# A decoder layer in split fp32: one 512-column product at the start of each gate, branch, out and down unit

## The chip, the cores and the metric

The kernel runs on one core of one Trainium2 chip. The metric is the device time of one execution in microseconds. The kernel before took 1376.24 us (median of three runs, 1376.17 to 1376.32).

## The reference

One layer of a decoder, 256 tokens of 2048 channels, all in float32. The large matrix products are the input projection, three branch projections, the output projection and the three of the FFN:

```python
h = rms_norm(x, norm_mix)
qkv..., gates = split_cols(h @ w_in, IN_SPLITS)      # 3608 columns, then 3 x 2048 gate columns
y_a, y_b, y_c = three attention mixers
merged = sum_i sigmoid(g_i) * (y_i @ w_br_i)
x = x + merged @ w_out
h = rms_norm(x, norm_ffn)
x = x + (silu(h @ w_gate) * (h @ w_up)) @ w_down     # width 5632
return rms_norm(x, norm_final)
```

## The kernel before

Each float32 operand of a large product is split into a high part in the fp32r format and a low part, the rest, also in fp32r; a product is then hi x hi + hi x lo + lo x hi. The activations are stationary (blocks of 128 channels by 128 tokens, two token tiles, `TT`), the weights are the moving operand.

The work goes in units. A unit is 256 rows (two blocks, `UK`) by 512 columns (`W`) of one weight matrix, 480 columns (`WQ`) in the first part. SyncE loads it into a ring of four slots (`raw_ring`), ScalarE writes the high part (`weight_hi_ring`, L1071), VectorE the low part (`weight_lo_ring`, L1322), and TensorE waits for the low part (`lo_ready`), multiplies, and counts `unit_used` up with its last product, which frees the slot.

The order of units is written out. First 64 units of the projection (query, key, value and so on; 480 columns, 248 in the last chunk), until about 170 us. Then, from unit `U_MIX` on, 96 gate units and 24 branch units, with the attention work placed between units by `follow` and `mixer_step`, and 32 out units, until about 660 us. Then the FFN: 88 gate, 88 up and 88 down units in an order of two halves (`ffn_plan`). Gate and up units alternate, with transposes of the activations between some of them (`act_transposes`). The up units have a scheme of their own (`up_unit`, `into`, L885 to L888), in which 55 of the 88 use seven block products for eight. The last four down units are multiplied in `last_units`.

All other units go through `products` (L636). For each of two blocks k, two token tiles t and two column halves, it issues three products of 256 columns: L646 hi x hi, L647 hi x lo, L648 lo x hi, with a weight load of the stationary block before each (PEld). Both halves of a token tile go to one PSUM bank, `bank[2 * pair + t]`; the first product into a bank of a chunk carries the start flag, and the second half relies on it (L645). `straight`, through `unit`, and `ffn_unit` call `products`.

Of the kernel before, what the change touches and what calls it, by code (L numbers as in the profile page):

```python
# [20 lines left out]
P = 128  # L21
TT = 2
# [3 lines left out]
W = 512  # L26
# [26 lines left out]
UK = 2  # L53
RING = 4
UPC = KD // UK
N_QKV = -(-N_PROJ // WQ)
U_MIX = N_QKV * UPC
# [65 lines left out]
LAST_DOWN = (1, NC_D - 1)  # L123
# [12 lines left out]
def half_of(i):  # L136

    return next(h for h, (a, b) in enumerate(HALVES) if a <= i < b)
# [93 lines left out]
def build_layer(nc, x_in, norm_mix, w_in, sinks, pe_k, w1_k, w2_k, pe_v, w1_v, w2_v,  # L232
                w_br_a, w_br_b, w_br_c, w_out, norm_ffn, w_gate, w_up, w_down, norm_final, out):
    ctx = ExitStack()
    with ctx:
# [3 lines left out]
        def at(name, shape, offset, dt=F32):  # L239
            return nc.alloc_sbuf_tensor_at(name, [P] + shape, dt, offset=offset)  # L240

        def place(name, shape, dt=F32):
            n = 4
            for s in shape:
                n *= s
            n = (n + 31) // 32 * 32
            t = at(name, shape, top[0], dt)
            top[0] += n
            assert top[0] <= nc.sbuf_top, name
            return t  # L250

        raw = place("raw_ring", [RING, UK, W])
        whi = place("weight_hi_ring", [RING, UK, W], F32R)
# [48 lines left out]
        h2T_hi = at("h2T_hi", [KD, S], mid, F32R)  # L302
        h2T_lo = at("h2T_lo", [KD, S], mid + 4 * KD * S, F32R)
# [52 lines left out]
        bank = [ctx.enter_context(nc.psum_tensor(f"bank{i}", [P, W], F32)) for i in range(8)]  # L356

        def sem(name):
            return ctx.enter_context(nc.semaphore(name))
# [5 lines left out]
        unit_used = sem("unit_used")  # L365
# [266 lines left out]
        def _(pe):  # L632
            def transpose(dst, src, n=P):
                return pe.transpose(dst, src, ident[0:n, 0:n])  # L634

            def products(slot, lhs, pair, first, last, k0, width=W, tiles=tuple(range(TT)), halves=(0, 1), apart=False):  # L636

                l_hi, l_lo = lhs
                parts = [(h * Q4, (h + 1) * Q4) for h in halves] if width == W else [(0, width)]
                for k, t, (a, b) in [(k, t, part) for k in range(UK) for t in tiles for part in parts]:  # L640
                    moved = apart and t == TT - 1 and a > 0
                    dst = bank[LAST_BANK][:, 0:Q4] if moved else bank[2 * pair + t][:, a:b]
                    x_hi, x_lo = (m[:, k0 + k, t * P:(t + 1) * P] for m in (l_hi, l_lo))
                    w_hi, w_lo = (m[:, slot, k, a:b] for m in (whi, wlo))
                    opening = first and k == 0 and (a == 0 or moved)  # L645
                    pe.matmul(dst, x_hi, w_hi, start=opening, stop=False, skip_group_check=True)  # L646
                    pe.matmul(dst, x_hi, w_lo, start=False, stop=False, skip_group_check=True)  # L647
                    m = pe.matmul(dst, x_lo, w_hi, start=False, stop=last and k == UK - 1, skip_group_check=True)  # L648
                return m

            def unit(u, lhs, q, j, n, width=W):

                pe.wait_ge(lo_ready, u + 1)
                m = products(u % RING, lhs, q % 2, j == 0, j == n - 1, UK * j, width)
                m.then_inc(unit_used, 1)

            def pair_free(q):

                if q >= 2:
                    how = evac_engine(q - 2)  # L660
                    pe.wait_ge(emptied[how], evac_count(q - 2))

            def straight(u):
                q, j = CHUNK_OF[u]
                kind, i, _, n = CHUNKS[q]
                if j == 0:
                    pair_free(q)
                    if q == 1:
                        pe.wait_ge(squares, 2 * NC_D)
                if kind == "branch":  # L670
                    s = i // NC_D

                    pe.wait_ge(values_read, (CMP + 1, N_SOFT, N_SOFT + SB_HEADS)[s])
                    lhs = (yT_hi[:, s % 2, :, :], yT_lo[:, s % 2, :, :])
                elif kind == "out":
                    lhs = (hT_hi, hT_lo)
                    if i == 0:
                        pe.wait_ge(t_lo, UPC + j + 1)
                else:
                    lhs = (hT_hi, hT_lo)  # L680
                    if q == 0:
                        pe.wait_ge(t_lo, j + 1)
                unit(u, lhs, q, j, n, min(WQ, N_PROJ - i * WQ) if kind == "qkv" else W)
# [210 lines left out]
            def up_unit(u, i, j):  # L894

                def block(k, t):
                    return tuple(m[:, UK * j + k, t * P:(t + 1) * P] for m in (h2T_hi, h2T_lo))

                stop = j == UPC - 1
                if not is_seven(u):  # L900
                    for k in range(UK):
                        into(i, 3, 0, block(k, 0), quarters(u, k, 0), stop)
                        into(i, 2, 0, block(k, 0), quarters(u, k, 1), stop)
                        into(i, 2, 1, block(k, 1), quarters(u, k, 0), stop)
                        m = into(i, 3, 1, block(k, 1), quarters(u, k, 1), stop)
                    return m
                n, e = SEVEN.index(j), N_SEVEN[u] % 2
                if i == 0:
                    pe.wait_ge(h_sum_lo, n + 1)

                def total(r):
                    return tuple(m[:, n, r, :] for m in (h2S_hi, h2S_lo))

                def extra(r):
                    return tuple(m[:, e, r, :] for m in (ext_hi, ext_lo))

                into(i, 6, 0, block(0, 0), quarters(u, 0, 0), True)
                into(i, 3, 0, block(1, 0), quarters(u, 1, 0), False)
                into(i, 2, 0, total(3), quarters(u, 1, 1), False)
                into(i, 6, 1, total(1), quarters(u, 0, 1), True)  # L920
                into(i, 7, 0, total(0), extra(0), True)
                into(i, 7, 1, total(2), extra(1), True)
                return into(i, 2, 1, block(1, 1), extra(2), False)

            def ffn_unit(u):

                what, i, j = FFN[u - U_FFN]
                if what == "gate":
                    if j == 0 and i == 0:
                        pair_free(Q_FFN)  # L930
                    elif j == 0 and half_of(i) != half_of(i - 1):
                        pe.wait_ge(added, TT * (NC_D - 1))
                    elif j == 0:
                        pe.wait_ge(silu_ready, i)
                    if i == 0:
                        pe.wait_ge(t_lo, 2 * UPC + j + 1)
                    pe.wait_ge(lo_ready, u + 1)
                    products(u % RING, (h2T_hi, h2T_lo), 0, j == 0, j == UPC - 1, UK * j).then_inc(unit_used, 1)
                elif what == "up":
                    if j == 0 and i == 0:  # L940
                        pair_free(Q_FFN + 1)
                        pe.wait_ge(squares, 2 * TT * NC_D)
                    elif j == 0:
                        pe.wait_ge(up_emptied, i)
                        if half_of(i) != half_of(i - 1):
                            pe.wait_ge(added, TT * NC_D)
                    pe.wait_ge(lo_ready, u + 1)
                    up_unit(u, i, j).then_inc(unit_used, 1)
                else:
                    h, c = i  # L950
                    n, done = KD_H[h], TT * (NC_D * h + c - 1)
                    if j == 0 and c == 0:
                        pe.wait_ge(silu_ready, HALVES[h][1])
                    elif j == 0 and c == 1:
                        pe.wait_ge(up_emptied, HALVES[h][1])
                    elif j == 0:
                        pe.wait_ge(added, done)
                    if c == 0:
                        pe.wait_ge(aT_lo, 2 * (HALVES[h][0] + j // 2 + 1))
                    if i == LAST_DOWN and j >= n - RING:  # L960
                        return
                    pe.wait_ge(lo_ready, u + 1)
                    products(u % RING, (actT_hi, actT_lo), c % 2, j == 0, j == n - 1, UK * j,
                             apart=i == LAST_DOWN).then_inc(unit_used, 1)

            def last_units():

# [45 lines left out]
            for u in range(UPC):  # L1013
# [14 lines left out]
                if u == 3:  # L1028
                    pe.wait_ge(rows_ready, 48)
                    pe.wait_ge(gains_ready, 1)  # L1030
                    for a in range(1, 4):
                        m = transpose(bank[2][:, KD * a:KD * (a + 1)], rows[0:KD, a, :], KD)
# [724 lines left out]
```

## Time and profile before

| | |
|---|---|
| median of the timed runs | 1376.24 us |
| the profiled execution, its own time | 1378.64 us |
| its span, first to last instruction | 1376.9 us |
| mean granted clock of TensorE | 0.999 |
| instructions of PE: products, weight loads | 11280, 11280 |
| products of L646 with 256 columns | 2624 |

The profile is one execution of the program. PE is TensorE's products, PEld its weight loads, which overlap the products, DVE is VectorE, ACT is ScalarE. The ends of products are modelled, so that the records of neighbouring products overlap; starts are as recorded. A line of the order of time gives start, duration, engine, line of the kernel, operation, written tile and read tiles, size, count of merged instructions, and in brackets an idle time before it. "128*128 128x256" is a stationary block of 128 by 128 and 256 moving columns. In a table of stretches the count behind a busy time (x...) is of all records that lie in the stretch, those over its edges included.

### The profile page before, as it was taken

The numbers are of one execution on the slowest core, as the hardware profiler recorded it, in microseconds if no ns is written. First come the engines' busy times: TensorE is split into PE (matmuls) and PEld (weight loads), VectorE is DVE, ScalarE is ACT, GpSimd is POOL, SyncE is SP. The second block draws the span as 40 slices with busy tenths as digits, with TensorE's granted clock in tenths as the row PEclk, the third lists the DMA queues.
The fourth block names the chain that finished last, engine by engine and source line by source line (L and its number), as shares of the span: only waits on it lengthen the run. The fifth ranks groups of instructions, "written<-read, shape, count | busy, mean of one in ns | idle before, by whom it ended". The sixth has DMA issues, their size and how long they took to land.

```text
span 1376.9 us, 26434 instructions
## 1 busy us (share of the span) xinstructions
PE 1362.5 (99%) x11280; PEld 1325.5 (96%) x11280; DVE 922.5 (67%) x1192; ACT 702.5 (51%) x913; POOL 44.9 (3%) x70
## 2 busy tenths in 40 slices
PE   8999999999999999999999999999999999999997
PEld 7888999999999999999999999999999999999997
DVE  5554557667655657666787888875446778887554
ACT  6343356656545655465645554544334455545444
POOL 3000010000000110000000000000000000000111
PEclk9999999999999999999999999999999999999999
DMA  7776655444565666546556655565555565666653
GB/s 241 246 231 219 186 171 156 140 152 146 154 192 168 194 203 218 184 168 201 165 182 194 217 181 181 182 214 208 191 198 184 184 214 169 193 196 231 210 198 123
DMA packets 135264, 261.08 MB, mean 190 GB/s; under 512 B 8448, under 2 KB 25408, under 8 KB 134768
## 3 DMA queue, kind: packets, MB, share of 16 engines
q1 hardware_dynamic: 132912, 251.13, 57.0%
q0 software_dynamic: 1792, 7.57, 1.6%
q8 instruction: 86, 1.41, 0.4%
q10 hardware_dynamic: 448, 0.76, 0.2%
q14 instruction: 26, 0.21, 0.0%
HBM read 257.33 MB, written 2.10 MB: 188 GB/s over the span
## 4 chain that ended last, share of the span: by engine, by line
PE 88%; DVE 7%; ACT 2%; DMA 2%; issue 1%; ACTq 0%; DVEq 0%
PE bank L646 24%; PE bank L647 23%; PE bank L648 23%; PE bank L885 4%; PE bank L887 4%; PE bank L888 4%; DVE weight_lo_ring L1322 2%; PE bank L634 2%; DVE weight_sums_lo L1342 1%; ACT weight_hi_ring L1071 1%; DMA raw_ring<-in_w_up 1%; DVE weight_sums L1331 1%; PE bank L784 1%; DVE act_rows L1382 1%; PE bank L695 1%
## 5 line engine op out<-in xcount | busy, mean ns | idle before, releaser
L1322 DVE TENSOR_TENSOR weight_lo_ring<-raw_ring,weight_hi_ring 128x1024 fp32r<-128x1024 f32 (+2 forms) x479 | 579.9, 1221 | 319.2 <-ACT weight_hi_ring L1071 263.9
L1071 ACT ACTIVATE weight_hi_ring<-raw_ring 128x1024 fp32r<-128x1024 f32 (+2 forms) x431 | 446.2, 1047 | 343.4 <-PE bank L648 271.0
L646 PE MATMUL bank<-weight_hi_ring,hT_hi 128*128 128x256 f32 (+2 forms) x1276 | 380.9, 298 | 0.0
L648 PE MATMUL bank<-weight_hi_ring,hT_lo 128*128 128x256 f32 (+2 forms) x1276 | 375.5, 294 | 0.0
L647 PE MATMUL bank<-weight_lo_ring,hT_hi 128*128 128x256 f32 (+2 forms) x1276 | 375.5, 294 | 0.0
L646 PEld LDWEIGHTS bank<-weight_hi_ring,hT_hi 128*128 128x128 f32 x1276 | 239.8, 188 | 10.0 <-issue 3.4
L647 PEld LDWEIGHTS bank<-weight_lo_ring,hT_hi 128*128 128x128 f32 x1276 | 239.9, 188 | 6.1
L648 PEld LDWEIGHTS bank<-weight_hi_ring,hT_lo 128*128 128x128 f32 x1276 | 239.6, 188 | 6.3
L646 PE MATMUL bank<-weight_hi_ring,h2T_hi 128*128 128x256 f32 x704 | 196.5, 279 | 3.2 <-DVE weight_lo_ring L1322 3.1
L648 PE MATMUL bank<-weight_hi_ring,h2T_lo 128*128 128x256 f32 x704 | 195.3, 277 | 0.0
L647 PE MATMUL bank<-weight_lo_ring,h2T_hi 128*128 128x256 f32 x704 | 195.3, 277 | 0.0
L646 PE MATMUL bank<-weight_hi_ring,actT_hi 128*128 128x256 f32 x704 | 194.5, 276 | 0.0
L647 PE MATMUL bank<-weight_lo_ring,actT_hi 128*128 128x256 f32 x704 | 194.3, 276 | 0.0
L648 PE MATMUL bank<-weight_hi_ring,actT_lo 128*128 128x256 f32 x704 | 194.3, 276 | 0.0
L646 PEld LDWEIGHTS bank<-weight_hi_ring,h2T_hi 128*128 128x128 f32 x704 | 132.5, 188 | 4.9 <-DVE weight_lo_ring L1322 4.0
L648 PEld LDWEIGHTS bank<-weight_hi_ring,h2T_lo 128*128 128x128 f32 x704 | 132.6, 188 | 0.0
L647 PEld LDWEIGHTS bank<-weight_lo_ring,h2T_hi 128*128 128x128 f32 x704 | 132.2, 188 | 0.0
L647 PEld LDWEIGHTS bank<-weight_lo_ring,actT_hi 128*128 128x128 f32 x704 | 132.1, 188 | 0.0
L646 PEld LDWEIGHTS bank<-weight_hi_ring,actT_hi 128*128 128x128 f32 x704 | 132.1, 188 | 0.0
L648 PEld LDWEIGHTS bank<-weight_hi_ring,actT_lo 128*128 128x128 f32 x704 | 132.1, 188 | 0.0
L1068 ACT ACTIVATE weight_sums_hi<-weight_sums 128x768 fp32r<-128x768 f32 x55 | 46.6, 847 | 129.8 <-DVE weight_sums L1334 71.4
L885 PE MATMUL bank<-weight_hi_ring,h2T_hi 128*128 128x256 f32 x374 | 105.5, 282 | 0.0
(253 smaller groups left out, 1897.0 us busy)
## 6 DMA issues: line engine op xcount, KB each, us to landing
raw_ring<-in_w_in SPq DMA_DIRECT2D x96, 512.0 KB, 3.4
raw_ring<-in_w_gate SPq DMA_DIRECT2D x88, 512.0 KB, 4.3
raw_ring<-in_w_up SPq DMA_DIRECT2D x88, 512.0 KB, 4.2
raw_ring<-in_w_down SPq DMA_DIRECT2D x88, 512.0 KB, 3.9
raw_ring<-in_w_in SPq DMA_DIRECT2D x55, 480.0 KB, 4.2
raw_ring<-in_w_out SPq DMA_DIRECT2D x32, 512.0 KB, 4.0
raw_ring<-in_w_br_c SPq DMA_DIRECT2D x16, 256.0 KB, 3.9
raw_ring<-in_w_br_a SPq DMA_DIRECT2D x16, 256.0 KB, 6.8
```

The source lines that it names most:

```text
L634: return pe.transpose(dst, src, ident[0:n, 0:n])
L646: pe.matmul(dst, x_hi, w_hi, start=opening, stop=False, skip_group_check=True)
L647: pe.matmul(dst, x_hi, w_lo, start=False, stop=False, skip_group_check=True)
L648: m = pe.matmul(dst, x_lo, w_hi, start=False, stop=last and k == UK - 1, skip_group_check=True)
L695: pe.matmul(dst[:, S:2 * S], v[0], pT[:, i % 2, h, 0:S], start=True, stop=False)
L784: m = pe.matmul(bank[4 + h][:, P * t:P * (2 * t + 1)], qT[half, pr, P * t:P * (t + 1)], keys[half, 0:P * (t + 1)], start=True, stop=True)
L885: pe.matmul(dst, l_hi, r_hi, start=(i, b) not in opened, stop=False, skip_group_check=True)
L887: pe.matmul(dst, l_hi, r_lo, start=False, stop=False, skip_group_check=True)
L888: return pe.matmul(dst, l_lo, r_hi, start=False, stop=stop, skip_group_check=True)
L1068: act.activation(ext_hi[:, n % 2, :, :], t_sum[:, :, :], ACT.Copy)
L1071: act.activation(whi[:, s, :, 0:width(u)], raw[:, s, :, 0:width(u)], ACT.Copy)\
L1322: dve.tensor_tensor(lo, w, hi.bitcast(F32), ALU.subtract).then_inc(lo_ready, 1)
```

## The change

`products` gets a flag, `whole`. With it, the unit begins with one hi x hi product of all 512 columns for the first block and the first token tile, and the two hi x hi products of 256 columns that it stands for are left out. The other 22 products follow in their old order. The flag is set for all units from `U_MIX` on that go through `unit`, for the FFN's gate units, and for the down units, but not in the up units, the projection's units and `last_units`.

```diff
-            def products(slot, lhs, pair, first, last, k0, width=W, tiles=tuple(range(TT)), halves=(0, 1), apart=False):
+            def products(slot, lhs, pair, first, last, k0, width=W, tiles=tuple(range(TT)), halves=(0, 1), apart=False, whole=False):

                 l_hi, l_lo = lhs
                 parts = [(h * Q4, (h + 1) * Q4) for h in halves] if width == W else [(0, width)]
+                if whole:
+                    pe.matmul(bank[2 * pair][:, :], l_hi[:, k0, 0:P], whi[:, slot, 0, :], start=first, stop=False,
+                              skip_group_check=True)
                 for k, t, (a, b) in [(k, t, part) for k in range(UK) for t in tiles for part in parts]:
...
-                    pe.matmul(dst, x_hi, w_hi, start=opening, stop=False, skip_group_check=True)
+                    if not whole or k > 0 or t > 0:
+                        pe.matmul(dst, x_hi, w_hi, start=opening, stop=False, skip_group_check=True)
                     pe.matmul(dst, x_hi, w_lo, start=False, stop=False, skip_group_check=True)
                     m = pe.matmul(dst, x_lo, w_hi, start=False, stop=last and k == UK - 1, skip_group_check=True)
                 return m
...
-                m = products(u % RING, lhs, q % 2, j == 0, j == n - 1, UK * j, width)
+                m = products(u % RING, lhs, q % 2, j == 0, j == n - 1, UK * j, width, whole=u >= U_MIX)
...
-                    products(u % RING, (h2T_hi, h2T_lo), 0, j == 0, j == UPC - 1, UK * j).then_inc(unit_used, 1)
+                    products(u % RING, (h2T_hi, h2T_lo), 0, j == 0, j == UPC - 1, UK * j,
+                             whole=u >= U_MIX).then_inc(unit_used, 1)
...
-                             apart=i == LAST_DOWN).then_inc(unit_used, 1)
+                             apart=i == LAST_DOWN, whole=u >= U_MIX).then_inc(unit_used, 1)
```

## Rows read from the trace of the kernel before

**Rows 1.** The page: engines (busy, share, instructions) and the span in 40 slices.
```profile
span 1376.9 us, 26434 instructions
PE 1362.5 (99%) x11280; PEld 1325.5 (96%) x11280; DVE 922.5 (67%) x1192; ACT 702.5 (51%) x913; POOL 44.9 (3%) x70
...
PEclk9999999999999999999999999999999999999999
DMA  7776655444565666546556655565555565666653
```

**Rows 2.** Waits of PE: who waited for whom, us in total, times, longest.
```profile
PE bank L646 <- DVE weight_lo_ring L1322: 3.1, 7, 1.1
```

**Rows 3.** The page's groups: busy us, mean ns of one, idle before.
```profile
L646 PE MATMUL bank<-weight_hi_ring,hT_hi 128*128 128x256 f32 (+2 forms) x1276 | 380.9, 298 | 0.0
L646 PE MATMUL bank<-weight_hi_ring,actT_hi 128*128 128x256 f32 x704 | 194.5, 276 | 0.0
```

**Rows 4.** Order of time, PE, in the down units at 1000 us.
```profile
999.83 0.28 PE L646 MATMUL bank<-weight_hi_ring,actT_hi 128*128 128x256 f32 x1
...
1001.98 0.28 PE L647 MATMUL bank<-weight_lo_ring,actT_hi 128*128 128x256 f32 x1
```

**Rows 5.** Order of time, PE, at 700 us, an up unit and the next gate unit.
```profile
699.75 0.28 PE L887 MATMUL bank<-weight_lo_ring,h2T_hi 128*128 128x256 f32 x1
...
700.58 0.28 PE L888 MATMUL bank<-weight_hi_ring,h2T_lo 128*128 128x256 f32 x1
700.70 0.28 PE L646 MATMUL bank<-weight_hi_ring,h2T_hi 128*128 128x256 f32 x1
...
701.99 0.28 PE L648 MATMUL bank<-weight_hi_ring,h2T_lo 128*128 128x256 f32 x1
```

**Rows 6.** Order of time, PE, around the transposes at 753.5 us.
```profile
753.40 0.28 PE L648 MATMUL bank<-weight_hi_ring,h2T_lo 128*128 128x256 f32 x1
753.52 1.03 PE L634 MATMUL bank<-identity,act_rows 128*128 128x128 f32 x8
...
754.52 0.28 PE L887 MATMUL bank<-weight_lo_ring,h2T_hi 128*128 128x256 f32 x1
...
755.20 0.28 PE L887 MATMUL bank<-weight_lo_ring,h_sums_hi 128*128 128x256 f32 x1
```

**Rows 7.** Stretches: length, busy time and records of each engine, clock, DMA share, GB/s.
```profile
674.00:709.00 35.00, 35.00 (x300) 35.00 (x299) 28.44 (x35) 18.71 (x21) 0.00 (x0) 1.00 0.62 196
711.00:753.00 42.00, 42.00 (x359) 42.00 (x358) 34.03 (x42) 21.71 (x25) 0.00 (x0) 1.00 0.60 189
866.00:884.00 18.00, 18.00 (x155) 18.00 (x155) 14.00 (x18) 7.58 (x8) 0.00 (x0) 1.00 0.61 205
886.00:893.00 7.00, 7.00 (x62) 7.00 (x61) 6.15 (x9) 3.99 (x6) 0.00 (x0) 1.00 0.58 195
1000.00:1100.00 100.00, 100.00 (x884) 100.00 (x884) 63.60 (x71) 45.11 (x46) 0.00 (x0) 1.00 0.59 190
...
90.00:150.00 60.00, 60.00 (x280) 52.12 (x279) 30.40 (x29) 23.54 (x24) 3.00 (x4) 1.00 0.69 216
```

**Rows 8.** Order of time, PE, behind attention work, at 228 and 277 us.
```profile
228.40 0.28 PE L647 MATMUL bank<-weight_lo_ring,hT_hi 128*128 128x256 f32 x1
...
228.87 0.28 PE L648 MATMUL bank<-weight_hi_ring,hT_lo 128*128 128x256 f32 x1
...
277.44 0.28 PE L647 MATMUL bank<-weight_lo_ring,hT_hi 128*128 128x256 f32 x1
...
277.67 0.28 PE L646 MATMUL bank<-weight_hi_ring,hT_hi 128*128 128x256 f32 x1
```

**Rows 9.** Order of time, PE, in the 480-column units at 120 us.
```profile
119.73 0.38 PE L646 MATMUL bank<-weight_hi_ring,hT_hi 128*128 128x480 f32 x1
119.96 0.38 PE L647 MATMUL bank<-weight_lo_ring,hT_hi 128*128 128x480 f32 x1
120.17 0.37 PE L648 MATMUL bank<-weight_hi_ring,hT_lo 128*128 128x480 f32 x1
```

**Rows 10.** Order of time, PE, at plain fp32 products and behind them.
```profile
473.66 0.59 PE L838 MATMUL bank<-probs_T,proj 128*128 128x256 f32 x2
474.09 0.38 PE L840 MATMUL bank<-probs_T,proj 128*128 128x128 f32 x2
...
474.44 0.28 PE L647 MATMUL bank<-weight_lo_ring,hT_hi 128*128 128x256 f32 x1
...
474.89 0.28 PE L648 MATMUL bank<-weight_hi_ring,hT_lo 128*128 128x256 f32 x1
```

## The prediction, made before the change was run

> **What bounds the kernel now.** I read the page first: PE is busy for 1362.5 of 1376.9 us, the granted clock is 9 tenths or more in every slice, and VectorE, ScalarE and the DMA engines are far from full [rows 1]. So the time is the sum of the distances from one product's start to the next. The waits of PE confirm it: seven waits for the low halves of the weights sum to 3.1 us, the longest 1.1 us [rows 2]. Then the order of time, because the durations in the groups (276 to 298 ns for a 256-column product, [rows 3]) are modelled ends and twice the true distance. What counts is start to start.
>
> That distance has two values for the same instruction. At 1000 us, 19 steps take 1001.98 - 999.83 = 2.15 us, 113.2 ns each; by the count of a long stretch, 100 us hold 884 products less about two that overlap the edges, 113.4 ns [rows 4, 7]. At 700 us, 19 steps take 701.99 - 699.75 = 2.24 us, 117.9 ns each [rows 5]; 42 us hold 359 less 2, 117.6 ns [rows 7]. I call these the quick and the slow rhythm. No wait is in either, both run across unit boundaries, and both run at the full granted clock, the 2.4 GHz level (its other level is 1.2 GHz). 256 columns at 2.4 GHz are 106.7 ns, so the quick rhythm loses 6.6 ns a product and the slow one 11. A rhythm once entered stays until something else passes through PE: the slow stretches of 674 to 709, 711 to 753, 866 to 884 and 886 to 893 us hold (300 + 359 + 155 + 62) products less the edges, 868, in 102 us [rows 7]. At 753.40 the eight transposes come, and 754.52 starts a quick stretch (six steps to 755.20, 113 ns each) [rows 6]. Of the 95 stretches of at least 12 unbroken products of 256 columns that I find in the order of time, 17 end in the slow rhythm and 78 in the quick one; [rows 8] show how an entry settles: 116 to 123 ns for two to four products, then 113.
>
> **The change part by part.** It touches 96 gate units and 24 branch units and 32 out units of the mixer part, 88 gate units and 84 down units of the FFN (the last four down units go through `last_units` without the flag): 324 units. In each, 24 products become 23: the first hi-by-hi product of 256 columns and the fourth, with the same stationary block, become one of 512. The arithmetic, the columns streamed and the bank are the same. The start flag, which the first half used to carry for the whole bank, is on the wide product. One weight load per unit goes. No wait, semaphore, DMA or other engine's instruction moves; the unit's one increment stays on its last product.
>
> *Price of the wide product.* Two products now cost 2 x 113.3 = 226.7 ns. No 512-column product is in the trace. The nearest row is the projection's 480 columns: 60 us hold 280 less 2 products, 216 ns each [rows 7], or 200 ns of columns and 16 of loss; single steps are 210 to 230 ns (119.73 to 119.96 to 120.17) [rows 9]. Carried on by the slope between 256 and 480 columns, (216.0 - 113.3) / 224 = 0.458 ns a column, 512 columns cost 230.7 ns: 4.0 ns more than the pair, 324 x 4.0 = +1.3 us. From the other side, the quick rhythm's loss of 6.6 ns may be paid once per product: 213.3 + 6.6 = 219.9 ns, 6.7 less than the pair, 324 x 6.7 = -2.2 us. The lowest row is a plain fp32 product of 256 columns, which is slower per column: two take 474.09 - 473.66 = 0.43 us, 215 ns each, just 2 ns over 512 column times [rows 10]. At 215 ns the pair is beaten by 11.7 ns, -3.8 us. The 480-column row is nearest in width and form, but its steps wander, so it is not settled as the 256-column rhythm is, and 512 is twice 256 where 480 is not. I take the middle of 219.9 and 230.7, 225.3 ns: -1.4 ns x 324 = -0.4 us. The ends, -3.8 and +1.3, stay for the range.
>
> The Trainium skill (TensorE: Matmul & The Clock Gate, Back-to-back issue gap) gives N / 2.4 + 2.5 ns for one product after another. By it the pair would be 218.3 ns, the wide product 215.8, and the change 324 x 2.5 = -0.8 us. The trace does not agree with it at 256 or 480 columns (113.3 against 109.2, 216 against 202.5) [rows 7], so no term of the sum rests on it.
>
> *Settling after the wide product.* It breaks the rhythm once a unit, as a transpose does. Entries after other work cost from nothing to about 22 ns over the quick rhythm: at 228.40, four steps to 228.87 take 0.47 us against 0.453, and at 277.44 two steps to 277.67 take 0.23 against 0.227 [rows 8] (to 10 ns, the rounding of a row; entry by entry I find about 3, 10 and 22 ns, 22 the most common in the mixer). Bounds: 0, if the wide product leaves the rhythm where it was, and 22 x 324 = +7.1 us. I take 0, because 512 columns are two whole products of the quick rhythm, and entries of 3 ns exist: behind the plain fp32 products at 474.09, four steps from 474.44 to 474.89 take 0.45 us, as in the quick rhythm [rows 10].
>
> *The slow rhythm ends sooner.* A wide product at the start of each gate or down unit is a new entry every 2.6 us, where the slow stretches now last 7 to 42 us. In the quick rhythm their 102 us would be 102 x 113.3 / 117.7 = 98.2, so 3.8 us can be had there. The first unit of each of the four stays as it falls, about 4 x 2.6 us x 0.037 = 0.4 us, and an up unit keeps what the unit before it left. I take -3.4 us. The other thirteen slow stretches, of 19 to 70 products, lie mostly in one unit; they are drawn anew, to no expected gain.
>
> *What hides what.* The ring of weights must keep up. In 711 to 753 us VectorE is busy 34.0 of 42 us [rows 7] and PE does not wait; a unit 4% shorter leaves it room (34 of 40.5). Where it would not, PE's waits [rows 2] grow from 3.1 us by at most the 3.4 us gained. I price that at nothing and keep it as a way to lose the gain.
>
> **Sum.** -0.4 + 0 - 3.4 = -3.8 us. The profiled execution took 1378.64 us, its span 1376.9; the median of the timed runs is 1376.24. The difference lies outside the change and I carry the sum over: 1376.24 - 3.8 = 1372.4 us.
>
> **The rivals.**
> (a) *The wide product is a plain stream*, 215 ns as the fp32 row: -3.8 - 3.4 = -7.2, 1369.0 us. For it: [rows 10]. Against it: fp32r rows of 480 columns lose 16 ns, not 2. The Trainium skill (Perfetto Trace Analysis, Matmuls) says larger matmuls are more efficient; the 480-column row, at 0.450 ns a column against 0.443 of the quick 256, speaks against it.
> (b) *Nothing is reset*: the rhythms go through the wide product unchanged, and only its price is left, -2.2 to +1.3 us: 1374.0 to 1377.5, about 1376. For it: both rhythms pass unit boundaries and go from L646 to L885 unharmed; against it: everything else of another shape does break them.
> (c) *It resets, and each reset must settle.* 22 ns behind each wide product and 230.7 ns for it: 324 x 26 = +8.4, less 3.4, +5.0: 1381.2 us, slower. For it: the commonest entry in the mixer [rows 8].
> (d) *The wide product leaves PE in the slow rhythm*, always, since each unit is alike. Some 9000 products of 256 columns follow (324 x 22 in the units, 1947 in the up units), 1258 of them slow already; 7800 x 4.4 ns = +34 us, some 1411 us. For it: entries end slow in 17 of 95 cases, and for one starting phase always. Against it: 78 of 95. It decides the sign from about 600 more slow products than now (2.75 us / 4.4 ns).
> (e) The change doing nothing at all can be left out: 324 instructions go.
>
> **How the numbers follow.** The forecast case (price between 219.9 and 230.7 ns, rhythm reset, little settling: 1370.6 to 1374.1) gets 0.40, (a) 0.12, (b) 0.20, (c) 0.15, (d) 0.13. A measurement of this kernel can tell about 0.2% from no change, 2.75 us: 1373.5 and 1379.0 are the limits. Faster: 0.32 of the forecast case and (a), 0.44. Same: 0.08 of the forecast case, (b), and 0.04 of (c), 0.32. Slower: 0.11 of (c) and (d), 0.24. The range goes from (a), 1369.0, to (c), 1381.2, and leaves out (d) and the far edges.
>
> **What would show it.** In the profile after, L646 has groups of 128x512 summing to 324, and PE has 10956 products. The distance behind a 512-column product is 220 to 231 ns if the price is right, and the products behind it stand at 113 ns at once (forecast), after two to four of 116 to 123 (c), or at 118 to the unit's end (d). A window of 711 to 753 us holds about 359 starts if the slow rhythm persists, some 365 to 370 if it ends (wide products count once). PE's waits for the low halves stay near 3 us. I am wrong if the wide product falls outside 215 to 231 ns, or if the share of slow products grows.

## The result, and the profile after

The changed kernel takes 1402.67 us (median of five runs, 1402.41 to 1403.74) against 1376.24 us: a ratio of 1.0197, with a 95% interval of 1.0186 to 1.0208. It is 26.4 us slower. The forecast was 3.8 us faster, and the range ended at 1381.2 us. The kernel before took 1375.44 to 1379.15 us in five executions beside it; on the chips of the experiments its medians lie 1.7 to 6.1 us higher, so the 26.4 us hold for these executions. Two executions in the whole case, one of the kernel before (1697 us) and one of `wide_phase_128` (2287 us), had a mean granted clock of 0.75 and 0.56, and they are left out of every median and range below.

The page after, in the lines that answer to [rows 1], with the waits of PE for the weights and the groups of the new product:

```profile
span 1400.8 us, 25786 instructions
PE 1389.2 (99%) x10956; PEld 1339.3 (96%) x10956; DVE 923.8 (66%) x1192; ACT 701.5 (50%) x913; POOL 44.8 (3%) x70
...
PEclk9999999999999999999999999999999999999999
```

```profile
PE bank L641 <- DVE weight_lo_ring L1327: 0.2, 1, 0.2
```

```profile
L641 PE MATMUL bank<-weight_hi_ring,hT_hi 128*128 128x512 f32 x128 | 55.5, 433 | 0.0
L641 PE MATMUL bank<-weight_hi_ring,h2T_hi 128*128 128x512 f32 x88 | 35.4, 402 | 0.3 <-DVE weight_lo_ring L1327 0.2
L641 PE MATMUL bank<-weight_hi_ring,actT_hi 128*128 128x512 f32 x84 | 33.6, 400 | 0.0
L641 PE MATMUL bank<-weight_hi_ring,yT_hi 128*128 128x512 f32 x24 | 10.1, 422 | 0.0
```

The edit did what it says: 128 + 88 + 84 + 24 = 324 wide products, 10956 products instead of 11280. The clock is as before, VectorE and ScalarE are busy for the same time as before to within 1.3 us, and PE waits less (0.2 us for 3.1 [rows 2]). PE has fewer products and is busy for 26.7 us more. So the distance from one product to the next has grown, without a wait for anybody. The order of time shows it. After, in the down units at 1000 us, where the kernel before ran at 113 ns [rows 4]:

```profile
999.90 0.40 PE L641 MATMUL bank<-weight_hi_ring,actT_hi 128*128 128x512 f32 x1
1000.14 0.28 PE L651 MATMUL bank<-weight_lo_ring,actT_hi 128*128 128x256 f32 x1
1000.25 0.28 PE L652 MATMUL bank<-weight_hi_ring,actT_lo 128*128 128x256 f32 x1
1000.37 0.28 PE L651 MATMUL bank<-weight_lo_ring,actT_hi 128*128 128x256 f32 x1
...
1002.61 0.28 PE L652 MATMUL bank<-weight_hi_ring,actT_lo 128*128 128x256 f32 x1
1002.73 0.40 PE L641 MATMUL bank<-weight_hi_ring,actT_hi 128*128 128x512 f32 x1
```

The wide product takes 0.24 us, and the 21 steps from 1000.14 to 1002.61 take 2.47 us, 117.6 ns each: the slow rhythm, to the unit's end, and on into the next. The stretch of [rows 7] from 1000 to 1100 us and the one of 370 to 430 us, first after, then before:

```profile
1000.00:1100.00 100.00, 100.00 (x820) 98.56 (x819) 57.67 (x60) 42.79 (x43) 0.00 (x0) 1.00 0.58 181
...
370.00:430.00 60.00, 60.00 (x491) 59.02 (x490) 28.44 (x26) 25.74 (x26) 0.00 (x0) 1.00 0.66 186
```

```profile
370.00:430.00 60.00, 60.00 (x530) 59.95 (x529) 29.46 (x28) 26.96 (x27) 0.00 (x0) 1.00 0.64 193
```

100 us hold 820 less 2 products, 35.6 units of 23, so a unit takes 2812 ns; with 884 less 2 it was 36.8 units of 24, 2721 ns. From the starts of all products, one by one: of the 256-column steps of up to 125 ns in the whole program, 8203 were quick (113 or 114 ns) and 1433 longer before; after, 1357 are quick and 7719 longer. Over 113.3 ns a product these steps lose 6.6 us before and 34.4 us after.

**Where the 23.9 us of span went** (1400.8 - 1376.9): narrow products (256 columns) +27.8 us; wide products (512 columns), of which 256 were undisturbed by other work or a wait, 1.9 us in all over the 226.7 ns of a pair, 234 ns in the mean; steps of over 125 ns, which are the waits and the first steps behind other work, 13.9 us over before and 8.8 after, so -5.1 us, of which 2.9 us are waits for weights (3.1 before, 0.2 after). The sum is +24.6 us; the rest, under 1 us, is in the single steps at either end of other work.

**Which wide product does what.** Sorted by the rhythm it meets, taking only those in an unbroken stream:

```
met in       distance behind it     left in     count
quick        225 or 226 ns          slow        34
slow         235 or 236 ns          slow        205
slow         230 to 234 ns          quick       16
```

Each of the 34 met in the quick rhythm costs what the pair cost, and the products behind it pay. Another 68 wide products stand directly behind other work or a wait; behind them 35 streams settled in the quick rhythm and 33 in the slow one, and that is where the quick 15% comes from. The freed ones have a pattern too. Of those met slow with a wide product before them in the same stream, 201 stayed slow and ten were freed, and all ten follow a wide product that stood directly behind other work or a wait. Where the wide product before was itself met in a stream with another before it, 186 of 186 stayed slow.

### The profile page after: what moved, and what is told of

Same layout as the page of the kernel before. It is cut to its first block, busy times and chain, and to the rows that moved or that the text cites. A ratio compares the mean times of both kernels' runs of the same rounds, so it can differ in the third digit from the quotient of the medians.

```text
span 1400.8 us, 25786 instructions
## 1 busy us (share of the span) xinstructions
PE 1389.2 (99%) x10956; PEld 1339.3 (96%) x10956; DVE 923.8 (66%) x1192; ACT 701.5 (50%) x913; POOL 44.8 (3%) x70
## 4 chain that ended last, share of the span: by engine, by line
PE 97%; DVE 1%; DMA 1%; ACT 1%; issue 0%; ACTq 0%; DVEq 0%
PE bank L651 25%; PE bank L652 25%; PE bank L650 20%; PE bank L641 6%; PE bank L889 5%; PE bank L891 5%; PE bank L892 5%; PE bank L634 2%; PE bank L788 1%; PE bank L699 1%; DMA raw_ring<-in_w_in 0%; DVE weight_lo_ring L1327 0%; DMA sigmoid_gates<-in_norm_mix 0%; PE bank L748 0%; ACT weight_hi_ring L1076 0%; PE bank L1012 0%
## 5 line engine op out<-in xcount | busy, mean ns | idle before, releaser
L650 PE MATMUL bank<-weight_hi_ring,hT_hi 128*128 128x256 f32 (+2 forms) x1020 | 307.4, 301 | 0.0
L650 PEld LDWEIGHTS bank<-weight_hi_ring,hT_hi 128*128 128x128 f32 x1020 | 193.5, 190 | 6.2
L651 PE MATMUL bank<-weight_lo_ring,h2T_hi 128*128 128x256 f32 x704 | 193.4, 280 | 0.0
L652 PE MATMUL bank<-weight_hi_ring,h2T_lo 128*128 128x256 f32 x704 | 193.3, 280 | 0.0
L650 PE MATMUL bank<-weight_hi_ring,actT_hi 128*128 128x256 f32 x536 | 150.6, 281 | 0.0
L650 PE MATMUL bank<-weight_hi_ring,h2T_hi 128*128 128x256 f32 x528 | 148.0, 280 | 0.0
L889 PE MATMUL bank<-weight_hi_ring,h2T_hi 128*128 128x256 f32 x374 | 106.2, 284 | 0.0
L891 PE MATMUL bank<-weight_lo_ring,h2T_hi 128*128 128x256 f32 x374 | 104.9, 280 | 0.0
L892 PE MATMUL bank<-weight_hi_ring,h2T_lo 128*128 128x256 f32 x374 | 104.9, 280 | 0.0
```

The source lines that it names most:

```text
L889: pe.matmul(dst, l_hi, r_hi, start=(i, b) not in opened, stop=False, skip_group_check=True)
L891: pe.matmul(dst, l_hi, r_lo, start=False, stop=False, skip_group_check=True)
L892: return pe.matmul(dst, l_lo, r_hi, start=False, stop=stop, skip_group_check=True)
```

## The experiments

Times of the kernel before on the chips of the experiments have medians of 1380.3, 1377.9 and 1382.3 us, with 1375.2 to 1392.6 us in the last batch (28 executions). That scatter is part of the subject and is taken up below. For differences of a few us I read the traces.

### Order against size: `two_of_256_first`

```diff
-                    pe.matmul(bank[2 * pair][:, :], l_hi[:, k0, 0:P], whi[:, slot, 0, :], start=first, stop=False,
-                              skip_group_check=True)
+                    for c0, c1 in ((0, 256), (256, 512)):
+                        pe.matmul(bank[2 * pair][:, c0:c1], l_hi[:, k0, 0:P], whi[:, slot, 0, c0:c1],
+                                  start=first and c0 == 0, stop=False, skip_group_check=True)
```

> The order of the changed kernel with its old size: each of the 324 units begins with two hi x hi products of 256 columns of the same stationary block, and goes on as the changed kernel does. 24 products and 24 weight loads a unit. Theory S (the single product of 512 columns, with one weight load for the time of two products, is what throws PE from the quick rhythm of 113.3 ns into the slow one of 117.8): quick rhythm kept, 1376 us within 2. Rival O (the order does it: two hi x hi products in a row, then the low part of the first half): about 1400 us, products at 117.8 ns from the first unit on.

Measured: 1379.21 us against 1380.3, ratio 0.9996 (0.9979 to 1.0013). That is 3 us above the 1376 expected, but no slower than the kernel before on this chip. Its stretch from 1000 to 1100 us:

```profile
1000.00:1100.00 100.00, 100.00 (x885) 100.00 (x884) 65.65 (x74) 44.41 (x47) 0.00 (x0) 1.00 0.62 189
```

That is the 884 of [rows 7], so the order is innocent. Its profiled execution, at 1375.49 us, happened to be nearly all quick (9086 steps against 544).

### One instruction: `one_wide`

```diff
-                             apart=i == LAST_DOWN, whole=u >= U_MIX).then_inc(unit_used, 1)
+                             apart=i == LAST_DOWN, whole=u == AT["down", (0, 1), 2]).then_inc(unit_used, 1)
```

(and the same at the two other calls, which this unit does not reach)

> The kernel before with a single product of 512 columns in the whole program, in the third unit of the down chunk (0, 1), near 951 us, inside the longest quick stretch (929 to 1102 us, 1519 products). Theory S with memory (the rhythm stays where the wide product leaves it): one instruction slows about 1330 products by 4.4 ns each until the transposes near 1102 us, +5.9 us, 1382.1 us; in the trace 113 ns before and 118 ns for 150 us after. Rival L (the loss is local to a unit with a wide product and paid anew in each): at most 22 x 4.4 ns = +0.1 us, 1376.3 us.

Measured: 1385.54 us, ratio 1.0034 (1.0017 to 1.0052), 5.2 us between the medians. The order of time around the one wide product:

```profile
950.23 0.28 PE L650 MATMUL bank<-weight_hi_ring,actT_hi 128*128 128x256 f32 x1
950.34 0.28 PE L651 MATMUL bank<-weight_lo_ring,actT_hi 128*128 128x256 f32 x1
950.45 0.28 PE L652 MATMUL bank<-weight_hi_ring,actT_lo 128*128 128x256 f32 x1
950.57 0.39 PE L641 MATMUL bank<-weight_hi_ring,actT_hi 128*128 128x512 f32 x1
950.79 0.28 PE L651 MATMUL bank<-weight_lo_ring,actT_hi 128*128 128x256 f32 x1
950.91 0.28 PE L652 MATMUL bank<-weight_hi_ring,actT_lo 128*128 128x256 f32 x1
951.03 0.28 PE L651 MATMUL bank<-weight_lo_ring,actT_hi 128*128 128x256 f32 x1
...
954.44 0.28 PE L650 MATMUL bank<-weight_hi_ring,actT_hi 128*128 128x256 f32 x1
```

The steps ahead of it are 113 ns; behind it 31 steps, from 950.79 to 954.44, take 3.65 us, 117.7 ns each. The stretches ahead of it and far behind it:

```profile
930.00:950.00 20.00, 20.00 (x178) 20.00 (x178) 11.33 (x12) 8.24 (x8) 0.00 (x0) 1.00 0.63 216
960.00:1095.00 135.00, 135.00 (x1149) 135.00 (x1148) 74.39 (x75) 55.76 (x56) 0.00 (x0) 1.00 0.60 189
```

20 us hold 178 less 2, 113.6 ns; 135 us hold 1149 less 2, 117.7 ns. The stream behind the wide product holds 1327 narrow products, until the transposes near 1107 us, and every one of them is slow (some 1330 were expected). One instruction, which itself takes no longer than the pair, slows PE for 156 us. This is the theory with memory, at its price, and it refutes the local one. The 5.2 us have an interval of 2.3 to 7.2 us, above the 0.1 us of rival L. In the traced execution, at 1386.12 us, three more long streams behind 1107 us are slow as well, 1010 products against 75 in the traced execution of before; the kernel is the same there, and no run says whether the wide product has a part in it.

### More of it: `all_wide`

```diff
+                rest = [(k, t, part) for k in range(UK) for t in tiles for part in parts]
                 if whole:
...
+                    wide = [(k, t, (0, W)) for k in range(UK) for t in tiles if not (apart and t == TT - 1)]
+                    rest = [(k, t, part) for k, t, part in rest if apart and t == TT - 1]
+                    rest = sorted(wide + rest)
+                for k, t, (a, b) in rest:
```

> In the 324 units all products have 512 columns (12 a unit instead of 24; in the last down chunk the second token tile keeps 256). What is the distance between products of 512 columns? Theory S: as behind the first wide one, where it is 226 ns from the quick rhythm and 236 from the slow one; a stream of them settles at one of the two, so 12 x 226 = 2712 or 12 x 236 = 2832 ns a unit against 2720 before: 1376 or 1376 + 324 x 0.11 = 1412 us. From the slope of the 480-column row (230.7 ns): +15.6 us, 1392 us. If one load per product is what sets the loss, 220 ns: -26 us, 1350 us.

Measured: 1394.55 us, ratio 1.0099 (1.0075 to 1.0124), nearest to the 1392 us from the slope of the 480-column row. The distances are neither 226 nor 236 ns throughout:

```profile
399.69 0.40 PE L651 MATMUL bank<-weight_hi_ring,hT_hi 128*128 128x512 f32 x1
399.92 0.39 PE L652 MATMUL bank<-weight_lo_ring,hT_hi 128*128 128x512 f32 x1
400.15 0.40 PE L653 MATMUL bank<-weight_hi_ring,hT_lo 128*128 128x512 f32 x1
...
401.79 0.39 PE L651 MATMUL bank<-weight_hi_ring,hT_hi 128*128 128x512 f32 x1
402.02 0.40 PE L652 MATMUL bank<-weight_lo_ring,hT_hi 128*128 128x512 f32 x1
```

Ten steps take 2.33 us, 233 ns each; one by one they alternate between 231 and 236. So a stream of 512-column products is 3% slower than pairs in the quick rhythm, with half the weight loads. The rule of the Trainium skill weighed in the prediction (Perfetto Trace Analysis, Matmuls: larger matmuls are more efficient) does not hold for these fp32r products from 256 to 512 columns at this placement of the tiles, and the measurement decides.

### An uneven pair: `split_384_128`

Against `two_of_256_first`:

```diff
-                    for c0, c1 in ((0, 256), (256, 512)):
+                    for c0, c1 in ((0, 384), (384, 512)):
```

> As the kernel with two hi x hi products of 256 columns first, but cut into 384 and 128 columns: the same columns, 24 loads, an uneven rhythm of loads. Theory S, sharpened to the gap in the weight loads (the load behind the 384-column product comes 160 ns after the one before, and the rhythm falls slow): about 1400 us. Rival: only 512 columns do it, 1376 us. Third outcome: the 128-column product acts as an entry and returns PE to the quick rhythm: 1372 to 1378 us.

Measured: 1399.92 us, ratio 1.0142 (1.0113 to 1.0171). The time is the one expected of the gap in the loads, but the reason is not the one stated:

```profile
401.56 0.28 PE L653 MATMUL bank<-weight_hi_ring,hT_lo 128*128 128x256 f32 x1
401.67 0.39 PE L642 MATMUL bank<-weight_hi_ring,hT_hi 128*128 128x384 f32 x2
401.90 0.33 PE L652 MATMUL bank<-weight_lo_ring,hT_hi 128*128 128x256 f32 x1
402.06 0.29 PE L653 MATMUL bank<-weight_hi_ring,hT_lo 128*128 128x256 f32 x1
402.19 0.28 PE L652 MATMUL bank<-weight_lo_ring,hT_hi 128*128 128x256 f32 x1
402.31 0.28 PE L653 MATMUL bank<-weight_hi_ring,hT_lo 128*128 128x256 f32 x1
402.42 0.28 PE L651 MATMUL bank<-weight_hi_ring,hT_hi 128*128 128x256 f32 x1
```

The 384 and the 128 columns take 0.23 us together, no more than the pair, but the 256-column product behind them takes 0.16 and the next 0.13; then the quick rhythm is back. Step by step 170 + 58 + 169 + 124 + 118 = 639 ns for 567, 72 ns x 324 = 23 us, paid on the spot. Of 324 such units 242 end quick, 216 of them from quick to quick. An uneven pair has another cost, local and each time anew, and a time alone would have passed for a proof of the wrong theory.

### A table of forms: `probe_forms`

In 48 down units the first block has one of the forms, and 18 others have four transposes ahead. Two of the forms are

```diff
+    "ww": [("hh", 0, 512), ("hl", 0, 512), ("lh", 0, 256), ("lh", 256, 512)],
+    "lh": [("hh", 0, 256), ("hl", 0, 256), ("hh", 256, 512), ("hl", 256, 512), ("lh", 0, 512)],
```

> The kernel before, with the first block (k = 0, first token tile) of 66 down units given in other forms, to see which forms carry PE from one rhythm into the other. In chunks (0, 1) to (0, 3): every second unit is preceded by four transposes of the identity into a bank that is not in use (an entry, quick in some 8 of 10 cases) and the unit behind it has the form under test. In chunks (1, 0) to (1, 2): a wide unit, then the form under test, so that it meets the slow rhythm. Forms: one, two or three products of 512 columns; the wide one last, or as lo x hi; the hi x hi pair cut at 128, 192, 224, 240, 248, 264, 272, 288, 320, 384, 448 or 480 columns. Theory S: every form with one 512-column product ends slow, from either rhythm; cuts with 256 columns or fewer behind each load keep the quick one. Theory G (what matters is when the next load may start): the cuts 384, 448 and 480, with a load free early, fall slow too. Theory A (both rhythms attract, and what counts is where the form leaves PE): the outcome differs from form to form and depends on the rhythm met. The time itself is of no matter; 324 - 33 fewer wide units than the changed kernel, about 1385 us.

One execution, at 1389.78 us. The steps from the form under test on, in ns, read from the starts:

```
form                    met quick                        met slow
one of 512              226, then slow                   231 (three), 233, 234: then quick
two of 512              226 236 118 114, then quick      -
three of 512            226 236 231, then slow           236 236 231, then slow
cut 320                 141 90 139 118 122 116, quick    147 90 141 118 122 116, quick
cut 288                 128 103 131 118 114, quick       -
cut 272                 121 110 119 120 119 118, quick   125 116 119 116 114, quick
cut 224                 100 148 122 116 114, quick       104 142, quick
cut 192                 86 169, then slow                90 169 118 117 115 115, quick
cut 448                 198 28 198, then slow            208 28 201 127 126 117, quick
```

The other cuts, at 240, 248, 264, 272, 384 and 480 columns, end quick from either rhythm where they were tried, and the cut at 128 ends quick from quick and slow from slow. So theory G fails: of the cuts 384, 448 and 480 met quick only 448 ends slow. Most outcomes rest on one or two units.

Theory S fails: two wide products in a row leave PE quick, and all five single ones met in the slow rhythm freed it, here the one as lo x hi:

```profile
1333.52 0.28 PE L688 MATMUL bank<-weight_hi_ring,actT_lo 128*128 128x256 f32 x1
1333.64 0.28 PE L676 MATMUL bank<-weight_hi_ring,actT_hi 128*128 128x256 f32 x1
...
1334.11 0.39 PE L676 MATMUL bank<-weight_hi_ring,actT_lo 128*128 128x512 f32 x1
1334.34 0.28 PE L686 MATMUL bank<-weight_hi_ring,actT_hi 128*128 128x256 f32 x1
...
1335.83 0.28 PE L687 MATMUL bank<-weight_lo_ring,actT_hi 128*128 128x256 f32 x1
1335.94 0.28 PE L688 MATMUL bank<-weight_hi_ring,actT_lo 128*128 128x256 f32 x1
```

The steps are 118 ns ahead of it, 233 at it and 113 behind. Theory A stands: both rhythms hold themselves, and what counts is where a form leaves PE. The slow rhythm, looked at step by step, mostly repeats every three products (118, 118, 117 ns; 353.3 in all), so where in that round a wide product falls should decide. In the changed kernel 22 narrow products lie between two wide ones, and an up unit adds 21 or 24, a multiple of three: always one over a multiple, and 235 or 236 ns in 201 of 211 cases. In the probe this one had 22 + 4 = 26 ahead of it, two over.

### The round of three: `wide_as_lo_hi` and `wide_alternating`

```diff
+    return "lh" if u >= U_MIX else None                      # wide_as_lo_hi
+    return ("w", "lh")[u % 2] if u >= U_MIX else None        # wide_alternating
```

> One wide product a unit as in the change, but it is the lo x hi pair and comes fifth in the unit. Theory A with the slow rhythm a round of three products (118, 118, 117 ns) in which the place of the wide one decides: from one wide product to the next there are 22 narrow ones here too, so it is met at the same place of the round as in the changed kernel, 236 ns and slow again: 1402 us within 3. Rival P (its place in the unit or its operand decides, as the same form at 1334 us of the probe, behind 26 narrow products, took 233 ns and ended quick): 1390 us or less.

Measured: 1405.07 us, ratio 1.0151 (1.0097 to 1.0205). The form that freed PE in the probe doesn't free it here, with 22 products between: 235 wide products met slow with 22 (or 43, 67, 70) narrow ones behind the last take 235 or 236 ns and stay slow. That refutes rival P. The time is 3 us above the figure, at the edge of what was expected: 93% of the narrow steps are slow, against 85% in the changed kernel.

> One wide product in each of the 324 units still, but in even units first and in odd ones fifth, so that between two wide products there are 26 and 18 narrow ones in turn (not 22 each). Theory A with the round of three: behind 26 (two over a multiple of three) it is met where it costs 233 ns and frees PE, behind 18 it is met quick, 226 ns, and throws it out again. Half of the products slow: about 1388 us. Theory S (every wide product ends slow): 1402 us.

Measured: 1393.40 us, ratio 1.0064 (1.0038 to 1.0090), 11.7 us less than `wide_as_lo_hi`, with the same 324 wide products evenly spaced. The outcome is on the side of theory A but 5 us above its figure: 5498 of 9020 narrow steps are slow, 61% and not a half. The units do not alternate everywhere as the expectation has it. Where gate and up units take turns, the up units shift the counts, and 71% are slow (665 to 930 us); in the down units of 930 to 1110 us it is 55%, in the out units 46%. The parts of 26 and 18 are also exchanged: the wide product behind 26 narrow ones is mostly met quick and throws PE out, and the one behind 18 frees it. All wide products met slow, with a wide one before them in the same stream, in the changed kernel, `wide_as_lo_hi` and `wide_alternating`, by the count of narrow products between:

```
narrow products between      over a multiple of three    freed    stayed slow
18, 63                       none                        77       0
26, 74                       two                         33       7
22, 43, 67, 70               one                         10       458
```

This is the best evidence that the place in the round decides, as it rests on outcomes one by one and not on a time. The stretch of `wide_alternating`, and then that of `wide_as_lo_hi`:

```profile
1000.00:1100.00 100.00, 100.00 (x836) 98.84 (x835) 58.03 (x61) 43.87 (x44) 0.00 (x0) 1.00 0.62 192
```

```profile
1000.00:1100.00 100.00, 100.00 (x820) 98.56 (x820) 56.29 (x59) 42.67 (x43) 0.00 (x0) 1.00 0.59 182
```

### Twice the change: `two_wide_a_unit`

```diff
+    return "ww" if u >= U_MIX else None
```

> Twice the change: in each of the 324 units the hi x hi and the hi x lo pair of the first block are both one product of 512 columns. Theory A (two rhythms that both hold themselves; a wide product met in the quick one costs 226 ns and leaves PE in the slow one, a second wide one right behind costs 236 ns and lets it back after 118 and 114): a unit costs 226 + 236 + 118 + 114 = 694 ns where six quick products cost 680, so + 14 ns x 324 = 4.5 us over an all-quick run (1375.5 us): 1380 us, over 20 us faster than with one wide product a unit. Rival W (each wide product does its harm by itself): at least 1402 us.

Measured: 1378.26 us (1377.21 to 1379.13), ratio 0.9963 (0.9933 to 0.9992) to the kernel before and 24 us below the changed kernel (on another chip), with 324 wide products more:

```profile
1001.55 0.39 PE L658 MATMUL bank<-weight_hi_ring,actT_hi 128*128 128x512 f32 x1
1001.78 0.40 PE L658 MATMUL bank<-weight_lo_ring,actT_hi 128*128 128x512 f32 x1
1002.01 0.39 PE L658 MATMUL bank<-weight_hi_ring,actT_lo 128*128 128x256 f32 x2
1002.24 0.28 PE L668 MATMUL bank<-weight_hi_ring,actT_hi 128*128 128x256 f32 x1
1002.36 0.28 PE L669 MATMUL bank<-weight_lo_ring,actT_hi 128*128 128x256 f32 x1
1002.47 0.28 PE L670 MATMUL bank<-weight_hi_ring,actT_lo 128*128 128x256 f32 x1
```

1002.24 - 1001.55 = 0.69 us for six products' worth, then 113 ns. This is the strongest test by time: the size was given ahead (1380), and if each wide product did its harm by itself, the time would be 1402 us or more.

### Freeing the old kernel: `reset_every_4th`

```diff
+    "c288": [("hh", 0, 288), ("hh", 288, 512)] + _REST,
+    return "c288" if u >= U_OUT and u % 4 == 2 else None
```

> The kernel before with a cut at 288 columns instead of 256 in the first hi x hi pair of every fourth unit number from the out units on (41 units). In the probe this form ended quick from the quick rhythm, at 128 + 103 + 131 + 118 ns for four products (27 ns over quick), and the cuts 272 and 264 from the slow one as well. If it frees PE from slow stretches: cost 41 x 27 ns = 1.1 us, gain the slow stretches of out and FFN beyond some 10 us each (4 us in the traced run of before, more in its later runs): 1376 to 1378 us, 2 to 4 us under the runs of before beside it, and less scatter. If it doesn't free: +1.1 us.

Measured: 1377.60 us (1376.26 to 1379.29), ratio 0.9960 (0.9934 to 0.9985). The gain on the median, 4.7 us, is above the 2 to 4 us given. In the trace 40 units have the form (the 41st falls to `last_units`, which does not use it), and behind every one PE is quick: 31 times from the quick rhythm, nine times from the slow one. The best runs of before (1375.2) stay 1.1 us below its best (1376.3), as 40 x 27 ns would have it. Where gate and up units take turns such a unit comes only every 44 us, so its trace still has 922 slow products there, against 1069 in the trace of before. It and `two_wide_a_unit` beat the kernel before and the changed one in the median, by holding every execution near the best time of before and not by going below it. That 12 runs lie within 3.0 us where before has 17 supports that before's scatter is the draw of its entries; the executions of before above 1380 us were not traced, so this reason for them is likely and not shown. What the traces of before, `one_wide` and this kernel have alike is the part up to 540 us, with 393 to 395 slow products each; from 1110 to 1300 us they have 75, 1010 and 377.

### The addresses: `wide_phase_384`, `old_phase_384`, `wide_phase_128`

```diff
-MOVING, STATIONARY = 128, 192
+MOVING, STATIONARY = 128, 384
```

> The changed kernel with the stationary tiles placed 256 bytes off the moving ones within each 512 bytes, instead of 64 (the constant STATIONARY 384 for 192). Theory M (the rhythms are the meeting of the moving read with the weight load at fixed addresses): both rhythms change their distance, and the time leaves 1402 us by over 5 us either way. Rival I (the rhythms are TensorE's own, whatever the addresses): 1402 us within 2, products at 113.3 and 117.8 ns.

> The kernel before with STATIONARY 384 for 192. Theory M: another time by over 5 us, and other distances than 113.3 and 117.8 ns. Rival I: 1376 to 1385 us, as the kernel before.

> The changed kernel with STATIONARY equal to MOVING (128): moving and stationary tiles begin at the same place within 512 bytes. Theory M: slower still than 1402 us, or at least other distances. Rival I: 1402 us within 2.

Measured: 1427.16 us for the changed kernel at 384, 1429.33 us for the kernel before at 384, 1427.63 us for the changed one at 128. The kernel before at 384:

```profile
1000.00:1100.00 100.00, 100.00 (x836) 100.00 (x835) 51.86 (x52) 38.27 (x38) 0.00 (x0) 1.00 0.57 181
```

100 us hold 836 less 2 products: 119.9 ns each, and of its 256-column steps 9068 are 120 ns and some 600 others 116 to 124, with no second rhythm that holds; PE waits for no weights in it. There the wide product does no harm: the changed kernel is 2.2 us faster than the unchanged one. So the two rhythms depend on how the tiles read as moving and as stationary operand lie to one another, 64 bytes apart within 512 in the kernel before, and the loss of this change is there at that placement and not at 256 bytes. At equal places the kernel before was not run, so what the change costs there is not known. Rival I is refuted. Of theory M it is borne out that the addresses set the distances; that the reads meet the weight loads is its reason and not shown.

## Why the prediction was wrong

**What bounds the kernel** was right: PE's distance from start to start, in a quick and a slow rhythm that outlive unit boundaries [rows 4, 5, 7].

**The price of the wide product** was right in the quick rhythm only: 225.3 ns taken, 226 measured in 34 cases. That it depends on the rhythm met was missed. 205 took 235 or 236 ns, outside the 215 to 231 that I had named as the sign of being wrong, and the mean is 234. The 256 undisturbed ones cost 1.9 us over the pairs. The section of the Trainium skill that I cited for N / 2.4 + 2.5 ns (TensorE: Matmul & The Clock Gate, Back-to-back issue gap) calls that the gap of an isolated product, which I left out, and for a stream of weight loads and products it gives 131 ns at 512 columns. The 233 ns measured in `all_wide` agree with neither figure.

**Settling after the wide product** is the step that failed: I put it at 0, and the wide product left PE in the slow rhythm instead of the quick one, which cost 27.8 us in the products behind. I bounded it by entries that settle back to 113 ns, 0 to 22 ns, and took 0 "because 512 columns are two whole products of the quick rhythm". A form may also not settle at all, and 34 of 34 met quick didn't. That two quick products are as long as 512 columns was no reason for the rhythm to go on. The 17 of 95 entries that end slow stood in the text, but I used them as a share over a crowd of unlike entries. Here the same form is repeated 324 times: it has nearly always one outcome, and a chance of 17 in 95 is then a chance of all or nothing, with an end of the range that belongs to it. The 0 and the middle of two bounds hid that I did not know the outcome.

**The slow rhythm ends sooner** (-3.4 us) has its sign turned round: +27.8 us. That slow stretches would be met by wide products was right, though in the gate units of the FFN, where the long slow stretches lie, only about every second unit has one, and not one each 2.6 us. But met in the same place of the round of three nearly every time, 205 of 221 stayed slow.

**What hides what** went unasked the other way: a slower PE gave back 5.1 us of waits and first steps.

**The rivals.** (d) is what happened, with its mechanism and its place. Its price was too large, 34 us for a measured 26.4: not all products fell slow (15% stayed quick, against the 0 I had counted) and the waits gave 5 us back. (a), (b) and (c) are refuted by the order of time after; the signs I had named for them and for (d) did tell them apart. The range left (d) out, as its chance of 0.13 allowed; the chance was wrong, not the arithmetic of the range.

## What to carry to other kernels

Where the order of time shows one instruction at two steady distances, without a wait, the engine may have states that hold themselves, as here, and an edit must be priced by the state in which it leaves the engine, not by its own length. If the same edit recurs at the same place, expect the same outcome each time: try it once, in a long steady stretch, and read the hundred microseconds behind it. And a kernel that has such states should be compared over many runs: the one before ranged over 17 us, likely by the rhythm that its streams fell into.

## What the runs showed of the hardware

- fp32r products of 256 columns, each with its own weight load, run at 113.3 ns or at 117.8 ns from start to start at the 2.4 GHz level when moving and stationary tiles lie 64 bytes apart within 512, and at 120 ns when they lie 256 apart (`old_phase_384`) or at equal places (`wide_phase_128`). At 64 bytes apart a product in a stream of 512 columns takes 233 ns (`all_wide`), of 480 columns 216 ns.
- A single 512-column product turned 113.6 into 117.7 ns for 156 us (`one_wide`). A second one right behind it turns it back, at 14 ns over six quick products (`two_wide_a_unit`).
- In the slow rhythm, a wide product 18 or 63 narrow ones behind the last freed PE 77 times in 77, one 22, 43, 67 or 70 behind it 10 times in 468.
- A product of 128 columns ahead of one of 256 costs 56 ns at the second (169 ns for 113), and at 64 and 32 columns more (198 and 200 ns; `split_384_128`, `probe_forms`).
- What in the reading of the two operands holds the rhythms, and why the slow one repeats every three products, stays open. No run here looks below the distances, and only three placements were tried.
